# Two fused transformer blocks: merges on split operands, layers written out, and each norm's chain in pieces of two chunks

## The chip, the cores and the metric
The kernel runs on one core of one Trainium2 chip. The time is device microseconds (us) of one execution; the figure for the kernel before is the median of three runs. KB are 1,024 bytes.

## The reference, cut to what matters
Two blocks on 256 tokens of width 1024. The first has two layers of this form:

```python
h = rmsnorm(x, norm_g)
proj = h @ w_in                       # 1024 x 11168, cut into 13 parts
y_a = ...                             # gated convolution, width 512
y_b = ... ; y_c = ...                 # two attentions with gates, width 512 each
g_a, g_b, g_c = jnp.split(jax.nn.sigmoid(gate_pre + b_gate), 3, axis=-1)
merged = g_a * (y_a @ w_out_a) + g_b * (y_b @ w_out_b) + g_c * (y_c @ w_out_c)
x = x + merged @ w_o
```

The second block is one layer: a norm of x and of a context of 256 tokens, modulated by vectors that come from `silu(c) @ w_ada`; attention; a second norm; and a mixture of 32 experts (1024 to 2048 to 1024) of which each token uses four. A last norm gives the result.

## The kernel before
Activations lie feature-major: 8 chunks of 128 features by 256 tokens (`x`, `h`, `conv`, `yB`, `yC`). Everything is float32. A large projection is made exact enough by splitting: each operand is a rounded part (float32r, `w_hi`, `h_hi`) and the rest (`w_lo`, `h_lo`), and PE sums three products, hi·hi, lo·hi and hi·lo.

**Work of a layer.** `UNITS` lists it: the lora part, dq, dk, dv and z by tokens (up to `PREP`), 20 units for the convolution and the gates (`PREP` to `FILL`), 12 merge units (`FILL` to `MERGED`; branch b over four pairs of output chunks p), 4 output units (two column halves by two pairs). Units end in one of four PSUM banks. Weights come in tiles of 2,048 KB (the first of a layer 1,664 KB) into two ring slots, one tile for every two units, one tile for each branch of the merges.

**Quarters.** For the projections a tile is split in four pieces of two chunks. For piece k ScalarE writes `w_hi` (L1794, `split_to`), GpSimd subtracts for `w_lo` (L1862) and PE multiplies (`quarter`, L1535 and L1545). There are three pieces (`PARTS`), so piece k waits until PE has used piece k-3. The merges of before don't split: PE multiplies the raw tile by `conv`, `yB` or `yC` (L1513), and VectorE gates and adds (L2023, L2027).

**Attention.** 24 jobs (8 of one attention, 16 of the other). In round j PE makes the scores of job j, then turns and multiplies the probabilities of job j-1, filling in quarters of the later units. VectorE in round j: `mask` (L2054), `divide`, `gated` for job j-1 (L2087). ScalarE: exponentials, copies of turned probabilities, the splits.

**Norms.** At a layer's start ScalarE squares x in two halves (L1808, into `squares_x`), PE sums the eight chunks by multiplying with `ones` (L1633, into PSUM `score`), VectorE makes the mean (L2098), ScalarE the root (L1813), VectorE the reciprocal (L2100) and eight products (L2102, `normed_x`); then for each half of four chunks ScalarE rounds (`stream_high`, L1802) and VectorE subtracts (`stream_low`, L1913). Before the output projection the merged sum goes through the same two steps, after the last merge unit. The second block's first norm (`modulated`, L1085 on) has the same chain and two passes over the chunks.

**Loads.** One queue (SyncE) issues all transfers in program order. At the start: constants (1,385 KB, with identity and ones), `cvec` (8 KB), x (1,024 KB), tiles 0 and 1 (1,664 and 2,048 KB). Then, once the layer before has ended, the layer's parameters (124.5 KB, L1454), the first half of an ada tile (1,024 KB, L1442), and the latent weights (768 and 512 KB). PE waits at its start for the constants, `cvec` and x. VectorE scales two of the parameters before it takes the mean. SyncE, PE, ScalarE, GpSimd and VectorE each run the layers in a hardware loop (`Fori(0, LAYERS)`).

**After the layers** comes the second block; its expert weights, 192 tiles of 2,048 KB, go through six ring slots.

## Time and profile before

| what | us |
|---|---|
| median of 3 runs | 2181.06 (2179.4 to 2181.25) |
| profiled execution, its time | 2179.23 |
| its span | 2177.4 |
| PE busy | 1989.5 (91%) |
| VectorE, ScalarE, GpSimd busy | 793.3, 520.5, 460.5 |
| moved by DMA | 563.4 MB, mean 259 GB/s |

The profile covers one execution, and times inside it count from the start of its span. PE is TensorE's matmuls, PEld its weight loads, DVE VectorE, ACT ScalarE, POOL GpSimd, SPq the SyncE queue's issues. A float32 matmul leaves two records, a split one leaves one. Matmuls overlap, so their record is longer than their step. "<-" behind an idle time names what ended it.

### The profile page before, as it was taken

To read this page: it belongs to the slowest core of one execution; us is meant where nothing else is said; L and a number is where in the kernel's file an instruction comes from. 1 tells how busy PE (TensorE), PEld (TensorE's weight loads), DVE (VectorE), ACT (ScalarE), POOL (GpSimd) and SP (SyncE) were. 2 spreads that over 40 slices of the span, in tenths; PEclk is the share of its full clock that TensorE was granted. 3 is DMA by queue.
4 is the path that set the end of the run, shared out by engine and by line. 5 is a ranking of instruction groups with operands and counts; after the bars stand their busy time and mean duration, and the time that the engine had idled before them with its cause. 6 is when DMAs were issued, how large, how long until landed. Compare 5 with 4: busy or idle time off the path is not lost.

```text
span 2177.4 us, 28592 instructions
## 1 busy us (share of the span) xinstructions
PE 1989.5 (91%) x10778; PEld 1258.0 (58%) x10778; DVE 793.3 (36%) x1604; ACT 520.5 (24%) x894; POOL 460.5 (21%) x196
## 2 busy tenths in 40 slices
PE   6989899979899899888997899999999999999997
PEld 5668889868679798863446544433333333333333
DVE  2785644234774633363454411111111111111112
ACT  3444345134454353111241100000000000000001
POOL 4566544047565442300000000000000000000000
PEclk9999999989999999998999799999999999999999
DMA  7455323345453332442144399999999999999994
GB/s 260 169 174 191 124 79 116 117 175 190 139 197 132 117 117 79 142 174 78 39 183 170 131 424 428 429 428 428 428 429 428 429 428 428 428 428 428 429 429 209
DMA packets 111422, 563.40 MB, mean 259 GB/s; under 512 B 4768, under 2 KB 24480, under 8 KB 86336
## 3 DMA queue, kind: packets, MB, share of 16 engines
q1 hardware_dynamic: 111328, 562.15, 64.6%
q8 instruction: 58, 0.95, 0.2%
q14 instruction: 36, 0.29, 0.0%
HBM read 561.08 MB, written 1.05 MB: 258 GB/s over the span
## 4 chain that ended last, share of the span: by engine, by line
PE 55%; DMA 30%; DVE 9%; issue 3%; ACT 2%; DVEq 0%; SPq 0%; ACTq 0%; PEldq 0%
DMA ring<-in_e_in_dram 29%; PE bank L1545 14%; PE score L816 9%; PE bank L1535 7%; PE bank L639 4%; PE bank L1513 4%; PE mixed L851 2%; PE mixed L1624 2%; PE score L1592 2%; PE bank L749 1%; PE flip L1607 1%; PE score L674 1%; DMA par<-in_layer_params_dram 1%; PE mixed L699 1%; PE flip L1568 1%
## 5 line engine op out<-in xcount | busy, mean ns | idle before, releaser
L1862 POOL TENSOR_TENSOR w_lo<-ring,w_hi 128x1024 fp32r<-128x1024 f32 (+1 forms) x192 | 460.3, 2406 | 466.3 <-ACT w_hi L1794 466.3
L816 PE MATMUL score<-ring,space 128*64 128x512 f32 x2048 | 461.6, 595 | 46.2 <-DMA ring<-in_e_in_dram 45.3
L816 PEld LDWEIGHTS score<-ring,space 128*64 128x64 f32 x2048 | 142.7, 137 | 353.8 <-issue 245.8
L1545 PE MATMUL bank<-h_hi,w_hi 128*128 128x256 f32 x896 | 263.1, 294 | 11.7 <-DVE h_lo L1913 11.7
L1794 ACT ACTIVATE w_hi<-ring 128x1024 fp32r<-128x1024 f32 (+1 forms) x192 | 200.3, 1048 | 285.0 <-PE bank L1545 135.8
L1545 PE MATMUL bank<-h_hi,w_lo 128*128 128x256 f32 x896 | 255.1, 285 | 0.0
L1545 PE MATMUL bank<-h_lo,w_hi 128*128 128x256 f32 x896 | 254.4, 284 | 0.0
L851 PE MATMUL mixed<-ring,space 128*64 128x512 f32 x1024 | 226.8, 596 | 0.0
L1033 ACT ACTIVATE space<-space 128x512 f32<-128x512 f32 x32 | 20.2, 631 | 719.1 <-DVE space L1334 719.1
L1545 PEld LDWEIGHTS bank<-h_hi,w_hi 128*128 128x128 f32 x896 | 173.8, 194 | 16.3 <-DVE h_lo L1913 12.5
L1334 DVE TENSOR_SCALAR space<-score 128x512 f32<-128x512 f32 x32 | 22.2, 693 | 432.1 <-PE score L816 432.1
L1545 PEld LDWEIGHTS bank<-h_lo,w_hi 128*128 128x128 f32 x896 | 172.7, 193 | 0.1
L1545 PEld LDWEIGHTS bank<-h_hi,w_lo 128*128 128x128 f32 x896 | 172.6, 193 | 0.0
L851 PEld LDWEIGHTS mixed<-ring,space 128*64 128x64 f32 x1024 | 70.8, 137 | 132.4 <-issue 130.5
L1535 PE MATMUL bank<-w_hi,h_hi 128*128 128x512 f32 (+1 forms) x320 | 135.0, 422 | 8.3 <-DVE h_lo L1913 8.3
L1347 DVE COPY space<-mixed 64x512 f32<-64x512 f32 x32 | 21.9, 684 | 295.6 <-PE mixed L851 295.6
L1535 PE MATMUL bank<-w_hi,h_lo 128*128 128x512 f32 (+1 forms) x320 | 128.0, 400 | 0.0
L1535 PE MATMUL bank<-w_lo,h_hi 128*128 128x512 f32 (+1 forms) x320 | 128.0, 400 | 0.0
L1535 PEld LDWEIGHTS bank<-w_hi,h_hi 128*128 128x128 f32 x320 | 63.0, 197 | 25.4 <-DVE h_lo L1913 9.6
L639 PE MATMUL bank<-ring,h 128*128 128x512 f32 (+1 forms) x160 | 68.0, 579 | 4.0 <-DVE h L1098 4.0
L1535 PEld LDWEIGHTS bank<-w_lo,h_hi 128*128 128x128 f32 x320 | 63.0, 197 | 13.0 <-issue 1.0
L1535 PEld LDWEIGHTS bank<-w_hi,h_lo 128*128 128x128 f32 x320 | 62.6, 196 | 13.3
(306 smaller groups left out, 2385.6 us busy)
## 6 DMA issues: line engine op xcount, KB each, us to landing
ring<-in_e_in_dram SPq DMA_DIRECT2D x128, 2048.0 KB, 25.2
ring<-in_e_out_dram SPq DMA_DIRECT2D x64, 2048.0 KB, 22.2
ring<-in_w_in_dram SPq DMA_DIRECT2D x42, 2048.0 KB, 7.8
ring<-in_w_ada_dram SPq DMA_DIRECT2D x16, 1024.0 KB, 5.2
ring<-in_w_o_dram SPq DMA_DIRECT2D x6, 2048.0 KB, 8.0
ring<-in_w_qkv_dram SPq DMA_DIRECT2D x4, 2048.0 KB, 9.6
ring<-in_w_ada_dram SPq DMA_DIRECT2D x4, 2048.0 KB, 8.2
ring<-in_w_out_a_dram SPq DMA_DIRECT2D x2, 2048.0 KB, 9.2
```

What stands on the lines that cost most here:

```text
L639: ins = pe.matmul(b[:, 0:n], src[:, c, tt * P:(tt + 1) * P], w8[:, c, 0:n], start=c == 0, stop=c == DC - 1)
L816: ins = pe.matmul(score[HALF * blk:HALF * blk + HALF, which * W:(which + 1) * W], xs[:, 2 * j + r, HALF * hh:HALF * hh + HALF], wk[:, blk ...
L851: ins = pe.matmul(mixed[HALF * side:HALF * side + HALF, :], actT[:, hh, a * P + HALF * half:a * P + HALF * half + HALF], ring[:, 4 + half, ...
L1334: dve.tensor_scalar(glu[:, hh, :], score[:, 0:W], GLU_LIMIT, None, ALU.min).then_inc(glu_free, 1)
L1347: dve.tensor_copy(ys[0:HALF, hh, :], mixed[0:HALF, :])
L1513: ins = pe.matmul(b[:, i * T:(i + 1) * T], w4[:, c, m:m + P], y[:, c, :], start=c == 0, stop=c == 3)
L1535: ins = pe.matmul(b[:, 0:n], x_[:, c, t], w_[:, k % PARTS, i, 0:n], start=c == 0 and x_ is h_hi and w_ is w_hi, stop=c == DC - 1 and x_ is ...
L1545: ins = pe.matmul(b[:, half * T:(half + 1) * T], w_[:, k % PARTS, i, m:m + P], x_[:, c, :], start=c == 0 and half == 0 and x_ is h_hi and ...
L1592: ins = pe.matmul(score[:, g * n:(g + 1) * n], q, k, start=True, stop=True)
L1624: ins = pe.matmul(o, v, pt[:, i * P:(i + 1) * P], start=first, stop=last)
L1794: act.activation(w_hi[:, k % PARTS, :, 0:n], ring[:, tl % LRING, :].rearrange("p (c n) -> p c n", c=DC)[:, 2 * q:2 * q + 2, 0:n], ACT.Copy ...
L1862: pool.tensor_tensor(w_lo[:, k % PARTS, :, 0:n], ring[:, tl % LRING, :].rearrange("p (c n) -> p c n", c=DC)[:, 2 * q:2 * q + 2, 0:n], w_hi ...
```

## The change
- **Merges are split.** The three merge tiles join `SPLIT`: unit p of a branch takes piece p (all four input chunks by 256 columns), rounded by ScalarE and subtracted by GpSimd. `conv`, `yB` and `yC` are rounded too: `round_branch` on ScalarE (after rounds 10 and 12 and after the jobs) and `low_branch` on VectorE (rounds 12 and 14 and after the jobs), into a new region `latent_r` over the latent q and k, and for `yC` into the upper half of `h_hi` and `h_lo`. PE's wait for `conv_ready` and for the last gate before the merges goes. The running total of a merge lies in PSUM (`score`, `flip`, `mixed`) instead of SBUF.
- **Norm chains in pieces of two chunks.** `squares_of_x`, `sums`, `stream_high` and `stream_low` work on four pieces. The merged sum's pieces are rounded as each is done. The squares and ones-matmuls of the next norm (the second block's first one too) start inside the output projection. `split_to` of pieces 0 to 2 is interleaved with the rounding, after the root.
- **Loads.** At the start: `cvec`, x in two halves, the parameters of both layers (249 KB), tile 0, ada's first half, tile 1, constants (now 1,321 KB), latent weights. `ones` is made by a memset. For layer two the ada half and the latent weights are asked for after the last merge unit. PE waits for the constants before its first projection.
- **Tables.** A dummy root on ScalarE before the first norm and before each layer's last splits. The square of the context waits for the second block's first sum.
- **Layers written out** instead of hardware loops; `mc` moves into `probs`.

```diff
 SPLIT = [(x[1], u) for u, x in enumerate(UNITS) if x[0] in ("lora", "dq", "dk", "dv", "z", "ac", "ax", "ab",
-                                                            "az", "gate", "out") and x[2][-1] == 0]
+                                                            "az", "gate", "out") and x[2][-1] == 0
+         or x[0] == "merge" and x[2][0] == 0]
 NQ = 4 * len(SPLIT)
 QUARTER = {u: 4 * i for i, (_, u) in enumerate(SPLIT)}
-NQ_PREP, NQ_FILL = QUARTER[PREP], QUARTER[MERGED]
+NQ_PREP, NQ_FILL, NQ_MERGED = QUARTER[PREP], QUARTER[FILL], QUARTER[MERGED]
 assert NQ % PARTS == 0
+
+NUSED = 3 * (NQ - NQ_MERGED + NQ_FILL) // 4
...
+        y_hi = [latent_r[:, 0:4, :], latent_r[:, 8:12, :], h_hi[:, 4:8, :]]
+        y_lo = [latent_r[:, 4:8, :], latent_r[:, 12:16, :], h_lo[:, 4:8, :]]
...
+            if UNITS[u][0] == "merge":
+                return ring[:, tl % LRING, :].rearrange("p (c n) -> p c n", c=4)[:, :, (k % 4) * T:(k % 4 + 1) * T]
+            n = LORA if k < 4 else W
+            return ring[:, tl % LRING, :].rearrange("p (c n) -> p c n", c=DC)[:, 2 * (k % 4):2 * (k % 4) + 2, 0:n]
+
+        def split_part(w, k):
+            if UNITS[SPLIT[k // 4][1]][0] == "merge":
+                return w[:, k % PARTS, :, :].rearrange("p a (b n) -> p (a b) n", b=2)
+            return w[:, k % PARTS, :, 0:LORA if k < 4 else W]
...
         def block_scalar(act):
-            act.wait_ge(free_of(NU - 1), freed(LAYERS - 1, NU - 1))
-            act.activation(h[:], x[:], ACT.Square).then_inc(bsquared, 1)
             act.wait_ge(bpar_loaded, 32)
+            act.wait_ge(scored, SCORE0 + 1)
             act.activation(hc, ctx_x, ACT.Square).then_inc(bsquared, 1)
...
+            sp.dma_start(cvec[:].rearrange("p c b -> p (c b)"), c_in).then_inc(c_loaded, 16)
+            for half in range(2):
+                sp.dma_start(x[:, 4 * half:4 * half + 4, :], xT[:, 4 * half:4 * half + 4, :]).then_inc(x_loaded[half], 16)
+            sp.dma_start(par[:, :], layer_params.rearrange("p a n -> p (a n)")).then_inc(par_loaded, 16)
...
+                    elif l:
+                        sp.wait_ge(free_of(MERGED - 1), freed(l - 1, MERGED - 1))
...
+                    if n == 0 and l == 0:
+                        ada_half(0, 0)
+                    if n == 1 and l == 0:
+                        sp.dma_start(cst[:], consts).then_inc(loaded, 16)
+                        latent_weights(0)
...
+                if l + 1 < LAYERS:
+                    ada_half(0, l + 1)
+                    latent_weights(l + 1)
...
+                    k = QUARTER[u - p] + p
+                    pe.wait_ge(lo_done, split_count(l, k))
+                    pe.wait_ge(y_ready, l * 3 + (2, 2, 3)[br])
+                    hi, lo = split_part(w_hi, k), split_part(w_lo, k)
                     for i in range(2):
-                        m = (2 * p + i) * P
+                        m = slice(i * P, (i + 1) * P)
                         for c in range(4):
-                            ins = pe.matmul(b[:, i * T:(i + 1) * T], w4[:, c, m:m + P], y[:, c, :],
-                                            start=c == 0, stop=c == 3)
+                            for y_, w_ in ((y_hi, hi), (y_lo, hi), (y_hi, lo)):
+                                ins = pe.matmul(b[:, i * T:(i + 1) * T], w_[:, c, m], y_[br][:, c, :],
+                                                start=c == 0 and i == 0 and y_ is y_hi and w_ is hi,
+                                                stop=c == 3 and w_ is lo, skip_group_check=True)
...
+                if kind in ("lora", "out"):
+                    pe.wait_ge(hready, l * 8 + (0 if kind == "lora" else 4) + q + 1)
...
+            def sums(l, pieces):
+
+                for i in pieces:
+                    if i == 0:
+                        pe.wait_ge(score_free, l * NS + 1)
+                    pe.wait_ge(squared, l * 4 + i + 1)
+                    for c in (2 * i, 2 * i + 1):
+                        ins = pe.matmul(score[:, 0:T], ones, squares_x[:, c, :], start=c == 0, stop=c == DC - 1)
+                    if i == 3:
+                        ins.then_inc(scored, 1)
+
+            pe.wait_ge(ones_ready, 1)
+            sums(0, range(2))
+            for l in range(LAYERS):
+                sums(l, range(2, 4))
+                if l == 0:
+                    pe.wait_ge(silu_ready, 1)
                 unit(l, 0)
+                if l == 0:
+                    pe.wait_ge(loaded, 16)
...
-                pe.wait_ge(conv_ready, l + 1)
-                pe.wait_ge(mixed_free, l * NM + NM + 1)
                 for u in range(FILL, MERGED):
                     unit(l, u)
                 for u in range(MERGED, NU, 2):
                     for q in range(4):
                         quarter(l, u, q)
+                        if u == NU - 2 and q == 1:
+                            sums(l + 1, range(2))
+            sums(LAYERS, range(2, 4))
...
+                    if NQ_FILL <= m < NQ_MERGED:
+                        act.wait_ge(unit_done, done(layer, SPLIT[m // 4][1] + m % 4))
...
+            def round_branch(l, br):
+                if br == 0:
+                    act.wait_ge(conv_ready, l + 1)
+                elif br == 1:
+                    act.wait_ge(scored, l * NS + MHEADS + 1)
+                    act.wait_ge(mixed_free, l * NM + MHEADS + 2)
+                else:
+                    act.wait_ge(unit_done, done(l, FILL - 1))
+                    act.wait_ge(mixed_free, l * NM + NM + 1)
+                act.activation(y_hi[br], (conv, yB, yC)[br], ACT.Copy).then_inc(y_rounded, 1)
...
+                piece = slice(2 * (n % 4), 2 * (n % 4) + 2)
+                act.wait_ge(stream_ready, l * 8 + n + 1)
+                if n == 6:
+                    act.wait_ge(unit_done, done(l, MERGED - 1))
+                act.activation(h_hi[:, piece, :], src[:, piece, :], ACT.Copy).then_inc(stream_hi, 1)
...
+            def squares_of_x(l, i):
+                if l:
+                    u = NU - 4 + i
+                    act.wait_ge(free_of(u), freed(l - 1, u))
+                else:
+                    act.wait_ge(x_loaded[i // 2], 16)
+                piece = slice(2 * i, 2 * i + 2)
+                act.activation(squares_x[:, piece, :], x[:, piece, :], ACT.Square).then_inc(squared, 1)
+
+            for i in range(4):
+                squares_of_x(0, i)
+            act.wait_ge(ones_ready, 1)
+            act.activation(stat[:, 0, 7:8], ones[:, 0:1], ACT.Sqrt)
+            act.wait_ge(par_ready, 1)
+            for l in range(LAYERS):
+                layer_now[0] = l
                 split[0] = 0
-                split_to(l, PARTS)
                 act.wait_ge(score_free, l * NS + 2)
                 act.activation(rsx, varx, ACT.Sqrt).then_inc(rsx_ready, 1)
-                act.wait_ge(par_ready, l + 1)
-                stream_high(l, 0, normed_x)
-                stream_high(l, 1, normed_x)
+                for n in range(4):
+                    split_to(l, min(n + 1, PARTS))
+                    stream_high(l, n, normed_x)
...
+                    if j in (10, 12):
+                        round_branch(l, 1 if j == 10 else 0)
+
+                round_branch(l, 2)
+                split_to(l, NQ_MERGED + 1)
+                stream_high(l, 4, merged_x)
+                split_to(l, NQ_MERGED + 2)
+                stream_high(l, 5, merged_x)
+                split_to(l, NQ_MERGED + PARTS)
+                stream_high(l, 6, merged_x)
+                stream_high(l, 7, merged_x)
+
+                act.activation(stat[:, 0, 7:8], ones[:, 0:1], ACT.Sqrt)
                 split_to(l, NQ)
+                for i in range(4):
+                    squares_of_x(l + 1, i)
...
+            def low_branch(l, n, br):
+                dve.wait_ge(y_rounded, l * 3 + n + 1)
+                dve.tensor_tensor(y_lo[br], (conv, yB, yC)[br], y_hi[br], ALU.subtract).then_inc(y_ready, 1)
...
+                    total = heads((score[:, 0:W], score[:, W:2 * W], flip[:, :], mixed[:, :])[p], T)
+                    dst = total if br == 0 else heads(mtmp, T)
...
-                    if br == 2 and p % 2 == 1:
+                        link(dve.tensor_tensor(total if br == 1 else merged_x[:, pair, :], total, heads(mtmp, T),
+                                               ALU.add))
+                    if br == 2:
                         dve.sem_inc(stream_ready, 1)
-                    if u == MERGED - 1:
-                        stream_low(l, 2, merged_x)
-                        stream_low(l, 3, merged_x)
+                        if p:
+                            stream_low(l, 3 + p, merged_x)
+                        if p == 3:
+                            stream_low(l, 7, merged_x)
...
-                for c in range(DC):
-                    ins = dve.scalar_tensor_tensor(out=normed_x[:, c, :], in0=x[:, c, :], scalar=l_("norm_g", c, 1),
-                                                   in1=rsx, op0=ALU.mult, op1=ALU.mult)
-                    if c % 4 == 3:
-                        ins.then_inc(stream_ready, 1)
-                stream_low(l, 0, normed_x)
-                stream_low(l, 1, normed_x)
+                for n in range(4):
+                    for c in (2 * n, 2 * n + 1):
+                        ins = dve.scalar_tensor_tensor(out=normed_x[:, c, :], in0=x[:, c, :], scalar=l_("norm_g", c, 1),
+                                                       in1=rsx, op0=ALU.mult, op1=ALU.mult)
+                    ins.then_inc(stream_ready, 1)
+                    if n:
+                        stream_low(l, n - 1, normed_x)
+                stream_low(l, 3, normed_x)
...
+                    if j in (12, 14):
+                        low_branch(l, j // 2 - 6, 1 if j == 12 else 0)
+                low_branch(l, 2, 2)
```

## Rows read from the trace of the kernel before

**Rows 1.** The page, part 2: the span in 40 slices, the DMA row

```profile
DMA  7455323345453332442144399999999999999994
```

**Rows 2.** Windows: stretch, its length, busy (instructions) PE PEld DVE ACT POOL, clock, DMA

```profile
440.93:446.55 5.62, 0.00 (x0) 0.00 (x0) 5.35 (x4) 1.06 (x1) 4.48 (x2) 0.68 0.74 255
446.55:470.90 24.35, 24.31 (x192) 24.11 (x192) 3.16 (x4) 6.37 (x6) 11.99 (x5) 0.93 0.22 76
470.90:488.60 17.70, 7.56 (x32) 5.35 (x32) 8.34 (x15) 7.42 (x9) 5.74 (x3) 0.77 0.96 346
901.80:907.75 5.95, 0.00 (x0) 0.00 (x0) 5.68 (x4) 1.06 (x1) 4.82 (x2) 0.95 0.80 268
931.94:948.35 16.41, 9.02 (x33) 7.07 (x33) 9.32 (x25) 5.50 (x5) 0.00 (x0) 0.89 1.03 371
```

**Rows 3.** The chain that ended last, four pieces of it: start, length, what

```profile
27.86 20.20 PE bank L1535 x84
...
365.73 2.82 PE bank L1545 x24
...
399.19 41.72 PE bank L1513 x192
...
471.09 9.15 DMA par<-in_layer_params_dram
```

**Rows 4.** Timeline, end of layer one's merges: start, length, instruction, idle before

```profile
437.53 7.88 POOL L1862 TENSOR_TENSOR w_lo<-ring,w_hi 128x1024 fp32r<-128x1024 f32 x3 [50.77 <-ACT w_hi L1794]
438.20 2.25 DVE L2027 TENSOR_TENSOR space<-space,ring 128x512 f32<-128x512 f32 x1
...
440.93 0.69 DVE L2023 SCALAR_TENSOR_TENSOR ring<-ring,bank 128x512 f32<-128x512 f32 x1 [0.48 <-PE bank L1513]
...
443.30 1.06 ACT L1802 ACTIVATE h_hi<-space 128x1024 fp32r<-128x1024 f32 x1 [3.00 <-DVEq L2029]
443.44 3.06 DVE L1913 TENSOR_TENSOR h_lo<-space,h_hi 128x1024 fp32r<-128x1024 f32 x1 [0.23 <-DVE space L2027]
```

**Rows 5.** Timeline, VectorE and GpSimd in rounds 12 and 14 of layer one

```profile
311.44 2.39 POOL L1862 TENSOR_TENSOR w_lo<-ring,w_hi 128x1024 fp32r<-128x1024 f32 x1 [2.07 <-ACT w_hi L1794]
...
325.40 0.28 DVE L2087 SCALAR_TENSOR_TENSOR space<-mixed,space 64x128 f32<-64x128 f32 x1 [5.11 <-PE mixed L1624]
...
325.73 2.38 POOL L1862 TENSOR_TENSOR w_lo<-ring,w_hi 128x1024 fp32r<-128x1024 f32 x1 [1.71 <-ACT w_hi L1794]
```

**Rows 6.** Timeline of the start, up to the first projection

```profile
12.11 5.77 PE L1633 MATMUL score<-space,cst 128*128 128x256 f32 x16 [12.11 <-ACT space L1808]
...
13.63 2.47 ACT L1794 ACTIVATE w_hi<-ring 128x832 fp32r<-128x832 f32 x3 [0.73 <-DMA ring<-in_w_in_dram]
14.61 5.74 POOL L1862 TENSOR_TENSOR w_lo<-ring,w_hi 128x832 fp32r<-128x832 f32 x3 [14.19 <-ACT w_hi L1794]
...
21.62 1.75 DVE L2100 RECIPROCAL ring<-ring 128x256 f32<-128x256 f32 x1 [0.48 <-ACT ring L1813]
...
22.47 1.36 PE L591 MATMUL mixed<-ring,silu 128*32 128x256 f32 x16 [4.59 <-DMA ring<-in_w_ada_dram]
23.41 3.26 DVE L2102 SCALAR_TENSOR_TENSOR space<-x,par,ring 128x256 f32<-128x256 f32 x8
...
26.58 2.43 DVE L1913 TENSOR_TENSOR h_lo<-space,h_hi 128x1024 fp32r<-128x1024 f32 x2
```

**Rows 7.** DMA view of 0 to 60 us, rate in 40 slices of 1.5 us

```profile
GB/s 0 199 384 396 420 394 400 407 405 395 386 387 351 348 388 406 208 310 348 8 0 0 0 0 67 355 416 388 172 11 5 44 350 408 399 215 281 382 25 0
```

**Rows 8.** Timeline, a table load of ScalarE, and the second block's first norm

```profile
190.26 1.28 ACT L1744 ACT_TABLE_LOAD   x1
191.55 0.60 ACT L1744 ACTIVATE ring<-bank 128x512 f32<-128x512 f32 x1
...
934.48 1.90 ACT L934 ACTIVATE space<-space 128x2048 f32<-128x2048 f32 x1
...
940.06 0.43 DVE L1085 TENSOR_SCALAR space<-score 128x256 f32<-128x256 f32 x1 [6.37 <-PE score L618]
```

More of the change, by code:

```diff
@@ L189 @@
 CP, NCP = places(CONSTS)
-CHAINED = dict(layer=177, pair=2, job=2)
+CHAINED = dict(layer=176, pair=2, job=2)
 def slope(g, h):
@@ L221, in build @@
         cst = sb("cst", [P, NCP])
+        ones = sb("ones", [P, P])[:]
         cvec = sb("cvec", [P, DC, 2])
@@ L260, in build @@
         stat = take(2, 8)
-        mc = take(4, MQK)
         probs = take(2, 1024)
@@ L380, in build @@
         par_ready = sem("par_ready")
+        c_loaded = sem("c_loaded")
+        x_loaded = [sem(f"x_loaded{i}") for i in range(2)]
+        ones_ready = sem("ones_ready")
         hi_done = sem("hi_done")
@@ L612, in place @@
                 return bank[u % BANKS], ring[:, BUNITS[u][1] % RING, :].rearrange("p (c n) -> p c n", c=DC)
-            for s, src in ((0, h[:]), (1, hc)):
-                pe.wait_ge(bsquared, s + 1)
-                pe.wait_ge(score_free, score_left(s))
-                for c in range(DC):
-                    ins = pe.matmul(score[:, 0:T], ones, src[:, c, :], start=c == 0, stop=c == DC - 1)
-                ins.then_inc(scored, 1)
+            pe.wait_ge(bsquared, 1)
+            pe.wait_ge(score_free, score_left(1))
+            for c in range(DC):
+                ins = pe.matmul(score[:, 0:T], ones, hc[:, c, :], start=c == 0, stop=c == DC - 1)
+            ins.then_inc(scored, 1)
             def project(u, parts=(0, 1)):
@@ L1625, in values @@
                 ins.then_inc(mixed_done, 1)
-            with pe.Fori(0, LAYERS) as l:
-                pe.wait_ge(score_free, l * NS + 1)
-                for c in range(DC):
-                    if c % 4 == 0:
-                        pe.wait_ge(squared, l * 2 + c // 4 + 1)
-                    ins = pe.matmul(score[:, 0:T], ones, squares_x[:, c, :], start=c == 0, stop=c == DC - 1)
-                ins.then_inc(scored, 1)
+            def sums(l, pieces):
[6 more added lines that the diff above has]
+                    if i == 3:
+                        ins.then_inc(scored, 1)
+            pe.wait_ge(ones_ready, 1)
[4 more added lines that the diff above has]
+                    pe.wait_ge(silu_ready, 1)
                 unit(l, 0)
+                if l == 0:
+                    pe.wait_ge(loaded, 16)
                 for u in range(HEAD, PREP):
@@ L1676, in _ @@
         def _(act):
-            act.wait_ge(loaded, 48)
+            act.wait_ge(c_loaded, 16)
             act.sem_inc(flip_free, 1)
@@ L1876, in link @@
                 dve.wait_ge(chain, base[0] + steps[0])
-            dve.wait_ge(loaded, 48)
+            dve.memset(ones, 1.0).then_inc(ones_ready, 1)
             for s in (score_free, mixed_free, squares_used, *bank_free):
```

125 lines of the change are left out of this document (53 added, 72 removed).

## The prediction
> **What bounds the kernel now.** I read four views in this order. First the page: its DMA row stands at 1 to 7 tenths until slice 23 and at 9 from slice 24 on [rows 1]. So there are two regimes: chains of the engines up to about 1237 us, then the stream of expert weights. I take it that a microsecond saved in the first is one saved at the end, because the stream's first transfers are released by the work before it and its amount doesn't change.
>
> Second, the table by stretch, with borders where TensorE (PE) stops and starts [rows 2]. The reader is to see where PE is empty: 0.00 of 5.62 us between the merges and the output projection, 0.00 of 5.95 in layer two, 7.56 of 17.70 at the border of the layers and 9.02 of 16.41 at the border to the second block. Beside these the start: PE's first projection is at 27.86.
>
> Third, the chain of waits [rows 3]. A quarter of a projection, 24 records of matmuls on split operands, takes 2.82 us; the twelve merge units, 16 float32 records each, take 41.72 without a stop. At the border of the layers the chain goes through the parameters (9.15 us), which are asked for only after the last output projection.
>
> Fourth, the timelines of the start, of the merges' end and of the second block's first norm, for the price of each step.
>
> **The change, part by part.** Differences are taken in the profiled execution, whose span is 2177.4 us and whose time is 2179.23, 0.1% under the median of 2181.06; I subtract them from the median.
>
> *Merges.* Each of a layer's twelve units becomes 24 split matmuls of the shape of the quarter in [rows 3] (128x128 weights, 256 columns). 12 x 2.83 = 34.0 us against 41.72, and PE's wait for the last gate before 399.19 (the chain's 0.5 us) goes, as the first eight units need only branches 0 and 1 rounded: -8.3 us a layer, **-16.6**. This holds if the two helpers keep up. A piece costs 1.06 on ScalarE (its copy of 1024 elements in [rows 4]) and 2.38 on GpSimd [rows 5], under 2.83; piece k may be written when unit k-3 is done, so it is ready 3.5 us later, while PE has 5.7 us of other units. VectorE has two instructions of 0.69 a unit, one operand in PSUM. The weights: tile 24 is asked for some 7 us into the merges; its 2,048 KB take 6 us at the rate below and are needed 19 us in.
>
> *VectorE beside GpSimd.* In [rows 4] a sum of two SBUF tiles of 512 elements takes 2.25 us, where an instruction of that size with one operand in PSUM takes 0.69; a difference of 1024 takes 3.06 there and 1.22 in [rows 6], where GpSimd is idle. Each ends 0.6 to 1.2 us, its own length, after a GpSimd instruction does (three in 7.88 us from 437.53, so at about 440.2, 442.8 and 445.4, the first a little earlier). So a VectorE instruction with two SBUF inputs that meets a running split waits for the rest of that split (0 to 2.4 us), and this I price. The Trainium skill, "SBUF — State Buffer", section "SBUF: two separate sides", has the rule, and it speaks against this change: the shared ports are an exclusive lock and the loser blocks fully. Under plain sharing of bandwidth I would add a few tenths; under the lock, the stalls below. The trace agrees with the lock.
>
> New such work: three differences of 128x1024 a layer (`low_branch`). The last is covered by the first eight merge units. The first two stand in jobs 12 and 14 right after `gated`, 1.2 us before the next mask, whose chain feeds PE's flips with almost no slack. In job 14 VectorE is free at 325.68 and GpSimd starts at 325.73, a tie; in job 12, one pair of 14.66 us earlier, VectorE is free at 311.02 and GpSimd starts at 311.44 [rows 5]: VectorE first. Winning costs 0.1, losing 2.4. I take 1.3 us a layer, **+2.6**; ends +0.2 and +10 (all four lose).
>
> *Gap before the output projection.* Call PE's end of the merges E. Chunks 0 and 1 of the merged sum are done 7.1 us earlier. ScalarE splits output piece 0 from E-5.7 to E-4.6 and rounds these chunks, GpSimd runs to E-2.2, the difference ends at about E-1.5: quarter 0 starts at E. The differences for quarters 1, 2 and 3 end at E+1.7, +4.8 and +5.5, locks priced in; PE wants them at +2.8, +5.7, +8.5. So -5.6 and -5.9: **-11.5**. A table load stands before split 3, whose GpSimd part ends at E+8.5, a tie: 0 to 1 us more.
>
> *Output projection.* 8 x 2.83 = 22.6 instead of 24.35 (it started on a granted clock of 0.93 on average, part of it at half clock [rows 2]), plus the first half of the next norm's sum, four float32 matmuls, 8 records at 41.72/192 = 0.217: 1.7. **0.0**: the sum costs here what the clock gives back.
>
> *Border of the layers.* From PE's end: VectorE 0.7, square of one piece 0.6, last two ones-matmuls 0.9, so the sum stands after 2.2. Then mean, root and reciprocal, 0.4, 0.4 and 1.75 [rows 6]. ScalarE splits piece 0 after the root; GpSimd's part (1.91) holds the ports until 3.85 after the sum; two normalizing products (0.41 each) end at 4.7, rounding at 5.3, the next two products at 5.5, the difference at 6.2. PE starts at 2.2 + 6.2 = 8.4. The second pair meets splits 1 and 2, and its difference ends at 11.7; quarter 0 is done at about 10.4. (Its length: 84 records, four quarters of 416 columns and three of 512, took 20.20 us in [rows 3]; at 2.3 and 2.8 they would be 17.6, so the first carries most of 2.6 us: 4.2.) So 1.3 us of stall: 17.70 - 8.4 - 1.3 = **-8.0**. Without locks 10.4 come back, with one more caught 5.6. The 9.15 us of the parameters go wholly, but the sum and the root's table had hidden in them.
>
> *Start.* The queue lands in order. Up to ada's first half 7,278 KB landed by 22.45, up to tile 0 4,081 KB by 13.6 [rows 6]: 361 KB a us. In the new order x (1,032 KB) is whole at about 5.5, the parameters at 6.2, tile 0 (2,945) at 10.5, ada (3,969) at 13.3. Squares, then 16 records at 0.36 make the sum stand at 11.0; quarter 0 could start at 17.2. But PE waits for the constants ahead of its first quarter, and they now stand behind tile 1: 7,338 KB, so 22.6. What is late next is the constants. 27.86 - 22.6 = **-5.3**; ends 0 and -10.7.
>
> *Border to the second block.* The mean starts 2.2 us after PE's end instead of 8.1 (931.94 to 940.06 [rows 8]). But ScalarE's square of the context (1.90) now waits for that sum and comes ahead of the root, and the root's table, loaded early by the dummy root, is displaced by the exponential of `lam` and loaded again, 2 x 1.28. The root ends 1.9 + 1.28 + 0.2 + 1.28 + 0.4 = 5.1 after the sum instead of 0.9: -5.9 + 4.2 = **-1.7**. The Trainium skill, "ScalarE: Activation LUTs", section "What ACT_TABLE_LOAD costs", adds a drain of 1.38 us to each load. In [rows 8] an activation starts 0.01 us after a load's end, so the trace doesn't show one; by the page this term would be +1.1.
>
> *At nothing:* unrolled loops (the same instructions in a row; PE's wait at the loop's end was for the parameters), `mc` moved, both layers' parameters in one transfer (249 KB, landed long before the mean), the latent weights (they land under the output projection; uncovered they would cost up to 3 us).
>
> **Sum.** -16.6 + 2.6 - 11.5 + 0.0 - 8.0 - 5.3 - 1.7 = -40.5. 2181.06 - 40.5 = **2140.6 us**.
>
> **Rivals.**
> A, *the lock costs more*: all four differences in the jobs lose (+7.4 over my value) and one more instruction is caught at the gap and at the border (2 x 2.4): 2153 us. For it: the ties above. Against it: VectorE is ahead in job 12.
> B, *the constants aren't late*: quarter 0 at 17.2 and 2135.2 us. For it: up to 420 GB/s in the first 20 us [rows 7]. Against it: the landings in order.
> C, *new waits replace the old one at the border*: quarter 0 still starts 17.7 us in, because splits, squares and rounding queue on ScalarE: 2148.6. Against it: they sum to 4 us.
> D, on the other side, *not faster*: GpSimd's subtract in the merges reads four runs of 256 columns of each partition instead of two of 512. If that slows it, a unit lasts as long as a piece: 24 x (d - 2.83) eats 40.5 us at d = 4.5; beyond it the kernel is slower, at 5.0 by 11.6 us, 2193. For it: no row shows this shape. Against it: 832 elements take 1.91 [rows 6] and 1024 take 2.38, in proportion to the elements.
> E, *none of it arrives*, as the expert stream's start is set by something else: 2181. Against it: before the stream DMA stands at 1 to 4 tenths [rows 1].
>
> **Chances and range.** Forecast 0.62 (2136 to 2147), A 0.14, C 0.08, B 0.11, D 0.03, E 0.02. Forecast, B, C and about half of A lie between 2130 and 2154, which also takes in the bounds that could fall together. 0.2%, 4.4 us, is about what a measurement here tells from no change. Faster 0.95, same 0.02, slower 0.03.
>
> **What would show it.** Right: merge units of 24 records and 2.83 us; no gap before the output projection; PE's first quarter near 22.6, released by the constants; two table loads before the second block's root; VectorE's differences ending after GpSimd's instructions. Wrong: GpSimd over 2.8 us an instruction in the merges and PE waiting for it, a first quarter far from 22.6, or an expert stream that starts no earlier.

## The result and the profile after

Median 2144.12 us (2142.3 to 2145.36) against 2181.15 us (2179.4 to 2183.8) of the kernel before on the same chip: ratio 0.9831, 95% interval [0.9819, 0.9843], 37.0 us faster. The forecast was 2140.6, 40.5 us faster. The profiled execution took 2145.36 us with a span of 2142.9, 34.5 under that of before.

The page of the changed kernel, its head and the DMA row of part 2:

```profile
span 2142.9 us, 27208 instructions
...
DMA  7545323355463233621172699999999999999994
```

Beside [rows 1] the stretch at 9 begins in the same slice, the 24th: a slice is 54 us long, too coarse for a move of 37 us. The move is seen in the first expert matmul, at 1193.50 us for 1230.25. From there to the end it is 949.40 us for 947.15, so the expert part moved as a block.

Windows of the changed kernel, from TensorE's (PE's) starts and stops (columns as in [rows 2]):

```profile
396.52:431.02 34.50, 34.50 (x291) 34.50 (x291) 16.54 (x22) 15.43 (x19) 28.13 (x12) 1.00 0.46 159
431.02:455.81 24.79, 24.78 (x201) 24.37 (x200) 6.63 (x8) 10.56 (x13) 14.99 (x7) 1.00 0.60 212
455.81:464.27 8.46, 3.24 (x24) 1.77 (x25) 6.06 (x9) 3.33 (x6) 1.94 (x2) 0.99 0.94 336
464.27:469.15 4.88, 4.01 (x12) 3.54 (x13) 4.88 (x4) 1.85 (x3) 4.19 (x2) 0.66 0.00 0
...
896.31:911.47 15.16, 7.65 (x25) 5.47 (x25) 9.33 (x25) 5.73 (x6) 0.00 (x0) 0.88 0.99 354
```

Merges are followed at once by the output projection: the two empty stretches of [rows 2] are gone. The 17.70 us of the border between the layers are 8.46, the 16.41 before the second block 15.16. GpSimd (POOL) works 28.13 of 34.50 us in the merges, 2.34 a piece, and holds nobody up.

The chain of waits of the changed kernel, four pieces:

```profile
8.55 14.90 DMA cst<-in_consts_dram
...
23.50 19.23 PE bank L1575 x84
...
363.38 2.87 PE bank L1585 x24
...
396.52 34.50 PE bank L1552 x288
```

The first quarter is released by the constants, as forecast, at 23.50. A quarter of 24 records takes 2.87 us where [rows 3] has 2.82, which was not expected. The first 84 records take 19.23 us where [rows 3] has 20.20. That is not the change: a second profile of the kernel before has 19.14 there, at a granted clock of 0.92 instead of 0.86.

Both profiled executions cut at PE's stops give the whole difference:

| stretch | before | after | difference | forecast |
|---|---|---|---|---|
| start to the first quarter | 27.86 | 23.50 | -4.4 | -5.3 |
| layer one, first quarter to the merges | 371.33 | 373.02 | +1.7 | +0.8 |
| merges, both layers | 83.49 | 69.00 | -14.5 | -15.6 |
| gaps before the output projections | 11.57 | 0 | -11.6 | -11.5 |
| output projections, both | 48.54 | 49.58 | +1.0 | 0.0 |
| border of the layers, to quarter 0 | 17.70 | 8.46 | -9.2 | -9.3 |
| layer two, quarter 0 to the merges | 371.45 | 372.75 | +1.3 | +2.1 |
| border to the second block | 16.41 | 15.16 | -1.2 | -1.7 |
| second block, to the first expert matmul | 281.90 | 282.03 | +0.1 | 0 |
| experts and end | 947.15 | 949.40 | +2.2 | 0 |
| sum | 2177.4 | 2142.9 | -34.5 | -40.5 |

The 2.2 us of the last stage are not the change either: written out and otherwise unchanged, the kernel before takes 949.9 us there, and the second profiles of both kernels, further below, take 947.2 and 947.5.

(In the forecast's column each layer's 1.3 us of locks and its 0.5 of the last gate's wait stand in the stretch up to the merges, and the stall of quarter 1 in layer two.)

### The profile page after: what moved, and what is told of

Same layout as the page of the kernel before. It is cut to its first block, busy times and chain, and to the rows that moved or that the text cites. A ratio compares the mean times of both kernels' runs of the same rounds, so it can differ in the third digit from the quotient of the medians.

```text
span 2142.9 us, 27208 instructions
## 1 busy us (share of the span) xinstructions
PE 1975.9 (92%) x10970; PEld 1255.2 (59%) x10970; DVE 802.3 (37%) x1619; ACT 555.2 (26%) x944; POOL 520.4 (24%) x220
## 4 chain that ended last, share of the span: by engine, by line
PE 55%; DMA 31%; DVE 9%; ACT 2%; issue 2%; SPq 0%; DVEq 0%; ACTq 0%
DMA ring<-in_e_in_dram 31%; PE bank L1585 14%; PE score L849 8%; PE bank L1575 8%; PE bank L672 4%; PE bank L1552 3%; PE mixed L1664 2%; PE mixed L884 2%; PE score L1632 2%; PE bank L782 1%; PE flip L1647 1%; PE score L707 1%; PE flip L1608 1%; DVE space L1978 1%; PE mixed L732 1%
## 5 line engine op out<-in xcount | busy, mean ns | idle before, releaser
L1943 POOL TENSOR_TENSOR w_lo<-ring,w_hi 128x1024 fp32r<-128x1024 f32 (+1 forms) x216 | 520.2, 2417 | 368.9 <-ACT w_hi L1847 368.6
L1847 ACT ACTIVATE w_hi<-ring 128x1024 fp32r<-128x1024 f32 (+1 forms) x216 | 226.3, 1049 | 238.2 <-PE bank L1585 130.5
```

Source lines behind the costliest of these rows:

```text
L1847: act.activation(split_part(w_hi, k), raw_part(k), ACT.Copy).then_inc(hi_done, 1)
L1943: pool.tensor_tensor(split_part(w_lo, k), raw_part(k), split_part(w_hi, k), ALU.subtract).then_inc(lo_done, 1)
```

## Experiments

### Do written-out loops cost anything
The kernel before with its five hardware loops replaced, all in this way:

```diff
-            with pe.Fori(0, LAYERS) as l:
+            for l in range(LAYERS):
```

> The kernel before with its five layer loops written out and nothing else changed. The changed kernel's split matmuls with 256 columns step 0.120 us apart where the kernel before has 0.118, so a quarter takes 2.86 to 2.88 us for 2.82 and about 2 us are lost in each layer. Theory 1, the straight code costs this: quarters of 2.87 us here too, and 3 to 5 us more, 2184 to 2186. Theory 2, it is where the operands lie in SBUF, which this kernel doesn't change: quarters of 2.82 and no difference, 2181 within 2. Prediction on record: writing out costs nothing.

2181.04 us, ratio to the kernel before 1.0005 (95% interval [0.9993, 1.0017]; such a pair of brackets stands behind every ratio below): no difference, and its chain keeps the old length of a quarter:

```profile
372.49 2.82 PE bank L1545 x24
```

So neither the loops nor the instructions' places in memory explain 2.87.

### Constants earlier
The changed kernel with the constants asked for right behind tile 0:

```diff
                     if n == 0 and l == 0:
+                        sp.dma_start(cst[:], consts).then_inc(loaded, 16)
                         ada_half(0, 0)
                     if n == 1 and l == 0:
-                        sp.dma_start(cst[:], consts).then_inc(loaded, 16)
                         latent_weights(0)
```

> The changed kernel with the constants asked for right after tile 0, ahead of ada's first half and tile 1. Theory of the prediction: PE's first quarter (23.5 us) is held by the constants alone. They would land at about 14.5 us, ada (5,290 KB) at 17.2, PE's ada rows end at 18.3 and the first quarter starts there: 5 us earlier. The second pair's difference (22.6 us) then holds the second quarter for at most 0.5 us. 2139.5 within 2. Rival: VectorE's chain beside GpSimd (the lock) is late as well and takes over, gain under 2 us, 2142 or more. Rival: the queue doesn't land in order and the constants' place hardly matters, 2144.

2139.88 us, ratio 0.9825 [0.9808, 0.9841]: inside the expected 2139.5 within 2, though the start gave 3.1 us and not 5. Its chain at the start:

```profile
4.14 14.16 DMA ring<-in_w_ada_dram
...
18.43 1.93 PE mixed L625 x16
20.37 4.82 PE bank L1575 x16
```

The first quarter is at 20.37, 3.1 us earlier, and the lead lasts to the end: every border from the merges (393.11 for 396.52) to the first expert matmul (1190.09 for 1193.50) is 3.4 us earlier. So the constants were the late transfer. What is late next is ada's first half, landed at 18.30, and PE's 16 small matmuls on it take 1.93 us, not the 1.1 that I had put.

### The root of x first in the second block
```diff
         def block_scalar(act):
+
+            def stream_root(n, s):
+                act.wait_ge(bvar, n)
+                act.activation(brsx, bvarx, ACT.Sqrt).then_inc(broot, 1)
+
+            stream_root(1, 0)
             act.wait_ge(bpar_loaded, 32)
             act.wait_ge(scored, SCORE0 + 1)
...
             act.activation(lam[:, 2:4], lam[:, 0:2], ACT.Exp).then_inc(lam_exp, 1)
...
-            stream_root(1, 0)
             stream_root(2, 1)
```

> The changed kernel, with ScalarE's first root of the second block taken before the square of the context and the exponential of lam. Theory: these three and two table loads stand in the chain for 4.2 us; from PE's end to its first projection 15.2 becomes 11.0 us, and the time 2140 within 1.5. Rival: the context's chain, now later, or PE's ones-matmuls for it take the place of the wait, and the gain is under 1.5 us, 2143 or more.

2143.54 us (2137.44 to 2150.93), ratio 0.9845 [0.9824, 0.9866]: not the 2140 expected, and the total can't tell it from the changed kernel. The trace can. First the changed kernel's timeline, then this one's:

```profile
898.95 1.91 ACT L966 ACTIVATE space<-space 128x2048 f32<-128x2048 f32 x1 [1.28 <-PE score L1674]
898.97 0.43 DVE L1117 TENSOR_SCALAR space<-score 128x256 f32<-128x256 f32 x1 [0.91 <-PE score L1674]
900.88 1.28 ACT L968 ACT_TABLE_LOAD   x1
...
902.17 0.20 ACT L968 ACTIVATE space<-space 128x2 f32<-128x2 f32 x1
902.39 1.28 ACT L972 ACT_TABLE_LOAD   x1
903.69 0.42 ACT L972 ACTIVATE space<-space 128x256 f32<-128x256 f32 x1
```

```profile
897.59 0.42 ACT L967 ACTIVATE space<-space 128x256 f32<-128x256 f32 x1 [1.82 <-DVEq L1119]
...
899.86 6.67 PE L651 MATMUL score<-space,ones 128*128 128x256 f32 x16 [2.90 <-ACT space L972]
...
903.12 2.19 DVE L1130 TENSOR_SCALAR h<-h,mod 128x256 f32<-128x256 f32 x8
...
906.37 10.89 PE L672 MATMUL bank<-ring,h 128*128 128x512 f32 x25
```

In the changed kernel the root stands behind a square, a load, the exponential and another load, and starts 4.7 us after the mean. Here it starts 0.5 us after it (897.07), and PE's first projection is 11.95 us after the last output record (894.42) instead of 15.16. These 3.2 us are still there at the first expert matmul: 293.6 us after the layers' end for 297.2. Of the 4.2 us expected, the last one went to what the rival named: VectorE has `h` ready at 905.31, but PE is at the ones-matmuls of the context's sum until 906.37.

### Where a quarter's 0.05 us come from
An unused tile of 28 bytes in front of `x` (tiles begin at multiples of 32) moves `x`, `h`, `h_hi` and what follows by 32 bytes, back to the remainder by 128 that they have in the kernel before:

```diff
+        shift = sb("shift", [P, 7])
         layer_now = [0]
```

> The changed kernel with an unused tile of 7 float32 ahead of x, so that x, h_hi and all behind them lie 32 bytes further and, modulo 64 bytes, where they lie in the kernel before. Theory 2 of the first kernel of this call (place in SBUF): quarters go from 2.87 back to 2.83 us and merges from 34.5 towards 34.0, together 3 to 4 us, 2140.5 within 1.5. Theory 1 (straight code): nothing changes, 2144 within 1.5.

2138.26 us, ratio 0.9803 [0.9787, 0.982]. Its chain, and under it the row of the changed kernel for the token projections:

```profile
373.55 2.83 PE bank L1586 x24
...
487.87 11.34 PE bank L1576 x48
```

```profile
488.96 11.13 PE bank L1575 x48
```

Both lengths return to those of before (2.82, and 11.33 for 48 records), the merges go from 34.50 to 34.11 and the 24 records of an output quarter from 2.88 to 2.83. So 32 bytes of placement in SBUF decide: at the one place the quarters of 256 columns with `h_hi` streamed are 1.7% longer, at the other those of 512 columns with the weights streamed are 1.9% longer. A layer has 48 of the first and 40 of the second beside its merges and output projection, so the shift gives -0.05 x 48 + 0.05 x 40 - 0.39 - 0.26, about -1.1 us a layer. That is an estimate from the rows, 2.1 us in all for the 3 to 4 expected, because the quarters of 512 columns get longer. The median is 5.9 us under the changed kernel's, but its runs go from 2136.54 to 2151.42, so the total neither confirms nor refutes it.

### GpSimd's subtracts at the border of the layers
This kernel leaves out the three subtracts of layer two's first weight tile, so `w_lo` keeps what it held:

```diff
+                    if l and k < PARTS:
+                        pool.sem_inc(lo_done, 1)
+                        continue
                     pool.tensor_tensor(split_part(w_lo, k), raw_part(k), split_part(w_hi, k),
                                        ALU.subtract).then_inc(lo_done, 1)
```

> The changed kernel without GpSimd's three subtracts of the first weight tile at the border of the layers (w_lo of that tile keeps old contents, so layer two's first unit is computed from wrong rests of the weights). Theory, VectorE's instructions with two SBUF inputs wait for a running subtract: VectorE's normalizing products and differences there come earlier, the first quarter stands about 7.5 us after PE's last output record instead of 8.4, and the second doesn't wait (0.9 us now); together 1.5 to 2 us in the trace, and nothing elsewhere. Rival, the two engines share the bandwidth and the chain of the norm alone sets the start: 8.4 and 0.9 as now. The median is expected 0 to 2 us under the changed kernel's.

2141.87 us (2135.89 to 2146.04), ratio 0.9798 [0.9767, 0.983]. Timeline of the changed kernel at the border:

```profile
460.12 1.93 POOL L1943 TENSOR_TENSOR w_lo<-ring,w_hi 128x832 fp32r<-128x832 f32 x1 [11.14 <-ACT w_hi L1847]
461.08 2.45 DVE L2194 SCALAR_TENSOR_TENSOR space<-x,par,ring 128x256 f32<-128x256 f32 x4
...
464.05 2.58 DVE L2194 SCALAR_TENSOR_TENSOR space<-x,par,ring 128x256 f32<-128x256 f32 x2
...
464.26 4.20 POOL L1943 TENSOR_TENSOR w_lo<-ring,w_hi 128x832 fp32r<-128x832 f32 x2 [2.20 <-ACT w_hi L1847]
464.27 0.68 PE L1575 MATMUL bank<-w_hi,h_hi 128*128 128x416 f32 x1 [4.92 <-DVE h_lo L1999]
...
466.55 2.45 DVE L1999 TENSOR_TENSOR h_lo<-space,h_hi 128x512 fp32r<-128x512 f32 x1
...
469.15 0.43 PE L1575 MATMUL bank<-w_hi,h_hi 128*128 128x416 f32 x1 [0.86 <-DVE h_lo L1999]
```

And without the subtracts:

```profile
458.06 1.67 DVE L2197 SCALAR_TENSOR_TENSOR space<-x,par,ring 128x256 f32<-128x256 f32 x4
...
460.25 0.88 DVE L2197 SCALAR_TENSOR_TENSOR space<-x,par,ring 128x256 f32<-128x256 f32 x2
...
460.48 0.69 PE L1575 MATMUL bank<-w_hi,h_hi 128*128 128x416 f32 x1 [4.16 <-POOLq L1944]
...
461.04 0.68 DVE L2002 TENSOR_TENSOR h_lo<-space,h_hi 128x512 fp32r<-128x512 f32 x1
```

The same VectorE (DVE) work takes 1.67, 0.88 and 0.68 us where it took 2.45, 2.58 and 2.45. Quarter 0 starts 7.70 us after the last output record (460.48 - 452.78) for 8.46, and quarter 1 follows 4.3 us later without a wait, for 4.88. So the locks are real and cost 1.35 us at this border, where I had expected 1.5 to 2. Two waits are gone, 0.76 before quarter 0 and 0.86 before quarter 1, but quarter 0 itself is 0.3 us longer: 4.30 us at a granted clock of 0.50, for 4.01 at 0.59, where its last three records already ran at the full clock.

### Merges as before, the rest as in the change
The merges multiply the raw tile again, and no branch is rounded or subtracted:

```diff
-                                                            "az", "gate", "out") and x[2][-1] == 0
-         or x[0] == "merge" and x[2][0] == 0]
+                                                            "az", "gate", "out") and x[2][-1] == 0]
...
-                            for y_, w_ in ((y_hi, hi), (y_lo, hi), (y_hi, lo)):
-                                ins = pe.matmul(b[:, i * T:(i + 1) * T], w_[:, c, m], y_[br][:, c, :],
...
+                            ins = pe.matmul(b[:, i * T:(i + 1) * T], w4[:, c, m:m + P], y[:, c, :],
+                                            start=c == 0, stop=c == 3)
```

> The changed kernel with its merges as before: unsplit, 16 float32 matmuls a unit on conv, yB and yC, PE waiting for the last gate, no rounding of the branches and no differences in the jobs; the norm chains, the loads and the pieces of the merged sum stay as in the change. Theory, the merges gave 7.2 us each by their matmuls and 0.5 by the wait, and the differences in the jobs cost nothing: merges of 41.7, both layers together +15.5, so about 2159.5. Rival, the differences in the jobs cost 1.3 us a layer as was predicted: +12.9, about 2157, and the jobs of this kernel 1.3 us a layer shorter than those of the changed one. A second rival, the split merges slow what comes after them (the first pieces of the output projection ready late): the output projection starts at once here too and is shorter, and less than 12 comes back.

2157.22 us, ratio 0.9879 [0.9851, 0.9908]. Its chain in layer two:

```profile
845.84 41.69 PE bank L1549 x192
```

From the merges' start to the last output record are 67.20 and 67.04 us in the two layers, for 59.29 and 59.29 in the changed kernel: +15.7 in all. The first theory's 15.5 is near for a reason that is in part another: 14.4 come from the matmuls, and 1.3 from the output projections, where PE now stands 0.5 and 0.4 us for a late piece; the wait for the last gate, 0.4 us a layer, lies ahead of these stretches and comes on top. PE goes from the merges into the output projection without a gap here too, so the pieces of the merged sum close the gap, not the split merges. The rounds are as long as in the changed kernel: from `gated` of round 12 (305.34) to the last one (393.91) 88.57 us, for 88.57 there. So the second rival is false, and the first one too, although its 2157 fits the median: the median shows 13.1 of the 15.7 because stretches that vary between executions, taken up below, add up the other way (layer one up to the merges -2.4, layer two +3.1, second block -1.2, experts -1.9).

### The differences in the jobs
This kernel leaves out VectorE's differences of the first two branches, and PE takes the rounded part in the place of the rest:

```diff
                     if j in (12, 14):
-                        low_branch(l, j // 2 - 6, 1 if j == 12 else 0)
+                        dve.wait_ge(y_rounded, l * 3 + j // 2 - 5)
+                        dve.sem_inc(y_ready, 1)
...
-        y_lo = [latent_r[:, 4:8, :], latent_r[:, 12:16, :], h_lo[:, 4:8, :]]
+        y_lo = [y_hi[0], y_hi[1], h_lo[:, 4:8, :]]
```

> The changed kernel without VectorE's two differences in rounds 12 and 14 of each layer; PE takes the rounded part of these branches in the place of their rest, so the merges do the same work on wrong rests. Theory, the two differences fall where VectorE has slack and GpSimd is idle or just starting: the rounds 12 to 16 take what they take now, to 0.2 us, no change. Rival, the lock of the prediction (1.3 us a layer): the later rounds come 1 to 1.5 us earlier after the round without the difference, and 2.6 us in all are gone. A second rival, the differences shift later splits and the price is paid in the rounds after 16: the same 1 to 3 us, but between round 16 and the merges.

2142.84 us (2138.01 to 2146.43), ratio 0.9805 [0.9775, 0.9834]. From `gated` of round 12 (306.92 here, 307.99 in the changed kernel) to the last `gated` before the merges (395.48, 396.56) are 88.56 and 88.57 us. The price is nothing. The changed kernel's timeline shows why:

```profile
308.32 1.22 DVE L2004 TENSOR_TENSOR latent_r<-space,latent_r 128x1024 fp32r<-128x1024 f32 x1
309.57 1.33 DVE L2148 SCALAR_TENSOR_TENSOR space<-cst,score 128x256 f32<-128x256 f32 x3
```

```profile
308.33 3.48 POOL L1943 TENSOR_TENSOR w_lo<-ring,w_hi 128x1024 fp32r<-128x1024 f32 x1 [1.74 <-ACT w_hi L1847]
...
323.11 3.34 POOL L1943 TENSOR_TENSOR w_lo<-ring,w_hi 128x1024 fp32r<-128x1024 f32 x1 [1.74 <-ACT w_hi L1847]
```

VectorE is first by 0.01 us in round 12 and by 0.13 in round 14, takes 1.22, and is done as the next mask's scores stand. GpSimd pays: 3.48 and 3.34 us where its neighbours take 2.40, and its idle time absorbs that. Without the difference its instruction in round 12 takes 2.38. VectorE got the ports in every case: both rounds of both layers in all seven profiles that have these differences. What a lost tie would cost was therefore never seen.

### The same kernels once more
The changed kernel and the kernel before, nothing edited.

> The changed kernel once more, nothing edited, for how far one execution stands for a kernel. Between kernels that run the same instructions there, three stretches differ: layer one from the first quarter to the merges took 369.6 to 373.0 us, layer two from its second quarter to the merges 367.9 to 371.9, and the second block from the end of the layers to the first expert matmul 296 to 298 or 305 to 306. Theory, this is where TensorE's half-clock stretches fall in an execution: this second profile of the same kernel differs from its first (373.0, 367.9, 297.2) in at least one of these by over 1 us, while the stages around the change (first quarter 23.5, merges 34.50, output projection 24.8, border 8.4 and 15.2) repeat to 0.3 us. Rival, each program has its own pattern, by its addresses or its issue order: all of them repeat to 0.3 us.

> The kernel before once more, nothing edited. Its first profile has 370.8 us from the first quarter to the last gate of layer one, and 298.3 in the second block; the copy with written-out layers had 372.0 and 305.9. Theory (half-clock stretches fall differently from one execution to the next): one of these differs here by over 1 us, and merges of 41.7, gaps of 5.6 and 5.9, borders of 17.7 and 16.4 repeat to 0.3 us. Rival, a pattern of each program: 370.8 and 298.3 again.

2142.96 us, ratio 0.9824 [0.9792, 0.9856], for the changed kernel, and 2176.71 in the one new run of the kernel before; spans 2141.5 and 2174.9. Both ran on another chip than the experiments above. The chains at the first merges:

```profile
396.05 34.50 PE bank L1552 x288
```

```profile
396.64 41.72 PE bank L1513 x192
```

Layer one up to the merges took the kernel before 369.0 us this time for 371.3 (396.64 - 27.65), and the changed kernel 372.6 for 373.0; layer two from its second quarter 369.0 for 367.9 in the changed kernel. So a program has no fixed pattern of its own, and the rivals of both expectations are false. The stages around the change repeat to 0.1 us in the changed kernel (merges 34.50, merges and output 59.29, border of the layers 8.46, border to the second block 15.2, first quarter 23.50) and to 0.2 in the kernel before. The second block did not move here (297.1 and 298.5), so these two runs alone don't show its second length of 305; nor did the stretch from the experts to the end stay as in the table: 947.45, 0.3 over before, not 2.2.

How two executions of one instruction sequence part is seen in the changed kernel and in the kernel without subtracts at the border, which are the same in layer one. Two pieces of each chain, and one window of each in the second block:

```profile
87.41 4.98 PE bank L1575 x12
...
211.21 4.36 PE bank L1585 x24
...
1111.47:1131.47 20.00, 18.53 (x90) 15.50 (x89) 9.46 (x5) 3.40 (x3) 0.00 (x0) 0.88 0.52 211
```

```profile
88.16 3.65 PE bank L1575 x12
...
208.98 2.87 PE bank L1585 x24
...
1104.80:1124.80 20.00, 18.53 (x61) 14.92 (x61) 9.46 (x5) 3.79 (x4) 0.00 (x0) 0.51 0.51 210
```

The same 12 records take 4.98 us at a granted clock of 0.53 or 3.65 at 0.75, the same 24 take 4.36 at 0.61 or 2.87 at 1.00, and the same place of the second block, 200 us behind its first projection, is passed at a granted clock of 0.88 or 0.51. The first two places are 2.8 of the 3.4 us between 373.0 and 369.6 in layer one; the second block is 297.2 us long in the one profile and 304.8 in the other. The chip isn't the cause: on the chip of the second one, the kernel with the constants earlier, with the same instructions in layer one, took 372.7 us there.

### Three edits together
Constants earlier, root first, and the 28-byte tile.

> The changed kernel with the constants asked for right behind the first tile, x's root of the second block ahead of the square of the context and the exponential, and 32 bytes in front of x. If the three gains are independent they add: 3.2 at the start, 3.4 at the border to the second block, 0.9 a layer by the placement, 8.4 in all, so about 2135.7. If the second one is caught up by the context's norm, or the expert stream's start doesn't follow, 2139.

2130.48 us (2126.92 to 2133.13), ratio 0.9761 [0.9738, 0.9784], some 13 us under the changed kernel, more than forecast. From the trace: first quarter at 20.23 (-3.3), merges and output 58.63 and 58.63 for 59.29 (-1.3), first projection of the second block 11.8 us after the layers for 15.2 (-3.4). These are 8.0 of the expected 8.4. Its span of 2125.0 is another 9.9 shorter, and 9.4 of these lie in the two stretches up to the merges (366.5 for 373.0, and 364.9 for 367.9). Placement explains under 1 of them. They are 2.5 and 2.9 us shorter than the shortest of any other profile, and whether that is chance or comes of the three edits wasn't tried.

## Why the prediction was right, and where it was off

The range and the sign held, and the mechanisms are those forecast. By steps:

- **Merges** (-16.6). Shown, with the size 1.1 us too large: 34.50 and not 34.0, because the 256-column quarter lasted 2.87 instead of 2.83. That GpSimd keeps up was right, so rival D is false: 2.34 us a piece in the new shape. Taking the split merges back gives 41.69 us again.
- **VectorE beside GpSimd** (+2.6). The step that failed is "I take 1.3 us a layer". The lock exists, but all ties went to VectorE, and without the differences nothing is gained (88.56 for 88.57). The term is 0.0; the ties were read rightly as ties, but the 1.3 picked between 0.2 for two won and 4.8 for two lost had no row behind it. Rival A falls with it. What the table has as +1.7 and +1.3 in these stretches is not it: the kernel before alone varies by 2.3 us there from one execution to another.
- **Gaps** (-11.5). Measured -11.6, and closed by the rounding in pieces: with the raw merges there is no gap either. The tie before split 3 cost nothing.
- **Output projection** (0.0). Measured +0.4 and +0.6. The sum's 8 records cost the 1.73 that I had put (1.7). The rest comes from quarters of 2.88 instead of 2.83, 8 x 0.05 = 0.4 a layer.
- **Border of the layers** (-8.0). Quarter 0 at 8.46 for 8.4 forecast; quarter 1 waits 0.86 for 1.3. The near hit of the first is two errors that cancel: the mean starts 2.58 us after the last output record for 2.2, and quarter 0 follows 5.88 later for 6.2. Without the subtracts the border gains 1.35 us, where I had 2.4 by the lock. The Trainium skill, "SBUF — State Buffer", section "SBUF: two separate sides", says the loser blocks fully. The trace agrees for each instruction (2.45 for 0.68). Rival C is false. What the earlier parameters gave and what the sum begun inside the output projection gave was not taken apart.
- **Start** (-5.3). Measured -4.4: the constants landed at 23.45 for 22.6, worked out with a rate taken from before. That the constants decide is shown by moving them. Rival B is false.
- **Border to the second block** (-1.7). Measured -1.2. The missing 0.5 is the sum again: the mean starts 2.66 us after the last output record (898.97 - 896.31) and not 2.2; from there to the root's end the forecast 5.1 took 5.1. The order of ScalarE's work is shown as its cause by putting the root first. The two loads take 1.28 us each and the activation starts 0.01 to 0.02 us after each. The Trainium skill, "ScalarE: Activation LUTs", section "What ACT_TABLE_LOAD costs", states a drain of 1.38 us for each load. It shows in no row here, as the prediction had taken it.
- **Loops written out at nothing.** Right: 1.0005. "Nothing" overlooked something else: moving tensors around changes the placement of `h_hi`, a cost of 1.1 us a layer by the rows, merges included.
- **The stream follows.** Right: the second block's 282.0 us for 281.9, and the expert part is equal to 0.3 us in the second pair of profiles. Rival E is false.

The terms as measured by the stages that repeat: start -4.4, merges -14.5, the last gate's waits -1.0 (0.5 each in the chain of before), gaps -11.6, output +1.0, border -8.3 (-9.2 and 0.9 of stall), second block -1.2: -40.0, against -40.5 forecast. That these are so near is luck in part: locks in the jobs priced at 2.6 that cost nothing, and 0.4 at the gaps and the border of the layers, make up for start, merges, output and second block, which together came out 3.5 too favourable in the forecast. The profiles show -34.5 and -33.4, the medians -37.0 (and -39.2 in the second comparison). Of the first pair's difference 2.2 lie in the expert part, which varies by that much without the change. Nearly all the rest of both is in the stretches up to the merges, where PE's clock falls differently in each execution and where, of the changes, only the placement is known to act. How much of the 1.7 and 1.3 us found there in the first pair, and of the 3.6 and 2.4 in the second, belongs to the changed kernel and how much to the executions stays open: with 369.0, 371.3 and 372.5 for the old order and 369.6 to 373.0 for the new one a cost of 1 us can't be told from none.

## What to carry to other kernels

Cut a large change into stages bounded by TensorE's stops and compare stage by stage, over two profiles of the same kernel: here stages without a clock change repeated to 0.1 us while the runs of one kernel spread over 3 to 15. A total that fits a theory can be chance: 2157.22 fitted the wrong one. When a wait is removed at the start, list the landings of everything asked for behind it, since the next transfer in the queue takes its place (constants, then ada). When a table-switching activation shares an engine with the step that releases TensorE, put that step first.

## What the hardware showed that was not expected

- Placement in SBUF changes a split matmul's step: with `h_hi` 32 bytes further, 24 records of 256 columns took 2.82 and not 2.87 us, and 48 records with the weights streamed 11.34 and not 11.13.
- The lock between VectorE and GpSimd holds both ways: a GpSimd subtract that started 0.01 us after VectorE's took 3.48 us, and 2.38 at the same place when VectorE's was left out.
- The same instruction sequence is granted different clocks at the same place: 0.88 or 0.51 over 20 us of the second block, which lasted 297.2 or 304.8 us; 373.0 or 369.6 us in layer one.
